# A fourth buffer in the ring of expert blocks for most of the last stage

## The reference, cut to what matters

```
def chunk(args):
    tc, ec, gc = args
    u_sel = expert_u[ec]
    a = jax.nn.gelu(jnp.einsum('cd,chkd->chk', tc, u_sel).astype(jnp.float32), approximate=False)
    w = (gc * a).astype(tc.dtype)
    return jnp.einsum('chk,chkd->cd', w, expert_v[ec])
```

## Time and profile before

| what | value |
|---|---|
| median of 3 timed runs | 1953.23 us |
| lowest and highest of them | 1952.56 and 1955.71 us |
| the profiled execution, its own time | 1951.24 us |
| its span, first to last instruction | 1949.3 us |
| busy: PE, DVE, ACT, POOL | 1940.0, 1664.4, 1122.1, 664.4 us |
| HBM traffic over the span | 290 GB/s |

### The profile page before, as it was taken

The page is one execution under the profiler, slowest core; times in us unless marked ns, Lnnn a source line. Parts: engine busy times, 40 slices in busy tenths (PEclk is TensorE's granted clock), DMA queues, the critical chain, the costliest instruction groups (busy, mean ns, idle before and its releaser), DMA issues.

```text
span 1949.3 us, 32645 instructions
## 1 busy us (share of the span) xinstructions
PE 1940.0 (100%) x11722; PEld 1765.4 (91%) x11722; DVE 1664.4 (85%) x2523; ACT 1122.1 (58%) x1589; POOL 664.4 (34%) x409
## 2 busy tenths in 40 slices
PE   9999999999999999999999999999999999999999
PEld 8899989998988888999999999999888888888887
DVE  8777778777888777999999999998888988888887
ACT  7565556555677455656665665655555455555555
POOL 0301110011000001887777877686222221333220
PEclk9999999999999999999999999999999999999999
DMA  6745654565455556999999999999999999999997
GB/s 246 252 160 194 204 191 159 188 204 194 162 173 192 185 173 228 336 341 341 334 334 341 345 326 355 336 384 356 358 364 387 381 374 371 381 376 381 371 379 270
DMA packets 137575, 566.50 MB, mean 291 GB/s; under 512 B 44008, under 2 KB 52080, under 8 KB 88112
## 3 DMA queue, kind: packets, MB, share of 16 engines
q1 hardware_dynamic: 87152, 414.05, 58.1%
q0 software_dynamic: 49936, 149.49, 22.9%
q10 hardware_dynamic: 432, 2.37, 0.3%
HBM read 548.31 MB, written 16.88 MB: 290 GB/s over the span
## 4 chain that ended last, share of the span: by engine, by line
PE 90%; DMA 4%; DVE 3%; ACT 1%; issue 1%; DVEq 0%; ACTq 0%; SPq 0%
PE psum L946 25%; PE psum L923 16%; PE psum L616 15%; PE psum L928 10%; PE psum L620 8%; PE psum L602 3%; PE psum L601 3%; PE psum L606 3%; DMA raw<-v_rows 2%; DMA arena<-u_cols 1%; ACT whi L479 1%; DVE xr L487 1%; DVE wlo L487 1%; PE psum L818 1%; PE psum L1000 0%
## 5 line engine op out<-in xcount | busy, mean ns | idle before, releaser
L473 DVE TENSOR_TENSOR wlo<-raw,whi 128x1024 fp32r<-128x1024 f32 x242 | 296.1, 1231 | 110.3 <-PE psum L620 72.2
L923 PE MATMUL psum<-xr,whi 128*128 128x384 f32 x2048 | 380.9, 337 | 0.0
L946 PE MATMUL psum<-whi,xr 128*128 128x512 f32 x1512 | 364.0, 390 | 0.3 <-DVE xr L1888 0.2
L923 PEld LDWEIGHTS psum<-xr,whi 128*128 128x128 f32 x2048 | 351.2, 188 | 0.5 <-ACT whi L479 0.2
L946 PEld LDWEIGHTS psum<-whi,xr 128*128 128x128 f32 x1512 | 283.6, 188 | 60.4 <-ACT whi L479 1.0
L479 ACT ACTIVATE whi<-raw 128x2048 fp32r<-128x2048 f32 x168 | 320.9, 1910 | 27.5 <-DMA raw<-v_rows 17.0
L616 PE MATMUL psum<-xr,whi 128*128 128x512 f32 x1296 | 330.2, 397 | 0.0
L466 ACT ACTIVATE whi<-raw 128x1024 fp32r<-128x1024 f32 x244 | 250.4, 1054 | 110.7 <-DMA raw<-stream 52.9
L1388 POOL DMA_INDIRECT arena<-v_rows,small x64 | 142.2, 2222 | 399.5 <-DVE arena L1852 396.0
L616 PEld LDWEIGHTS psum<-xr,whi 128*128 128x128 f32 x1296 | 232.6, 189 | 43.6 <-issue 0.2
L487 DVE TENSOR_TENSOR wlo<-raw,whi 128x1024 fp32r<-128x1024 f32 (+1 forms) x126 | 197.6, 1573 | 23.4 <-issue 19.9
(11 more groups left out here) (283 smaller groups left out, 3236.4 us busy)
## 6 DMA issues: line engine op xcount, KB each, us to landing
raw<-stream SPq DMA_DIRECT2D x244, 512.0 KB, 3.3
raw<-v_rows SPq DMA_DIRECT2D x85, 1024.0 KB
raw<-u_cols SPq DMA_DIRECT2D x84, 1024.0 KB
arena<-v_rows SPq DMA_DIRECT2D x43, 1024.0 KB, 7.9
arena<-u_cols SPq DMA_DIRECT2D x42, 1024.0 KB, 6.8
gates<-arena POOLq DMA_DIRECT2D x8, 1536.0 KB, 9.7
small<-gates SPq DMA_DIRECT2D x62, 192.0 KB, 8.2
arena<-x_t SPq DMA_DIRECT2D x4, 544.0 KB, 6.6
```

The costliest lines, as they stand in the source:

```text
L473: nc.vector.tensor_tensor(wlo[:, k % 2 * HALF:(k % 2 + 1) * HALF], raw[:, s * HALF:(s + 1) * HALF], f(whi[:, s * HALF:(s + 1) * HALF]), AL ...
L923: mm(bank(at, 0, 2 * TD), hi_w[:, c * P:(c + 1) * P], z_all[:, :, c, 0:TD // TS, :], start=c == 0, stop=False)
L946: last = mm(at[:, (b * 4 + j * 2 + n) * 512:(b * 4 + j * 2 + n + 1) * 512], weights, src, start=begin, stop=end, skip_group_check=True)
```

## The change

From block 144 on (block 16 of the V stage) the ring has a fourth slot, the first 2048 columns of arena, which held weight chunks that are used up by then. Blocks up to 143 keep their slots. Block 144 goes to the new slot, 145 to slot 0, 146 to 1, 147 to 2, 148 to the new one again, and so on. In SP's loop the turn n = 140 loads blocks 143 and 144; every later turn loads block n + 4 in place of n + 3. The waits for a block's load count the loads of its slot with a function, since a slot's count is no longer a quotient of the block's number.

```
-        slots = [raw[:, 0:D], raw[:, D:2 * D], top.take(D)]
+        slots = [raw[:, 0:D], raw[:, D:2 * D], top.take(D), arena[:, 0:D]]
+        DEEPER = F_V - F_U + 16
+
+        def slot(b):
+            return b % 3 if b < DEEPER else (3, 0, 1, 2)[(b - DEEPER) % 4]
+
+        def loads(b):
+            s = slot(b)
+            return sum(slot(a) == s for a in range(2, b + 1)) if s == 2 else sum(slot(a) == s for a in range(3, b + 1))
...
-        block_landed = [sem(f"block_landed{s}") for s in range(3)]
+        block_landed = [sem(f"block_landed{s}") for s in range(4)]
...
         def hi_block(act, b):
-            act.wait_ge(block_landed[b % 3], 16 * (b // 3 + (b % 3 == 2)))
-            nc.scalar.activation(whi[:, b % 2 * D:(b % 2 + 1) * D], slots[b % 3], ACT.Copy).then_inc(hi_done, 2)
+            act.wait_ge(block_landed[slot(b)], 16 * loads(b))
+            nc.scalar.activation(whi[:, b % 2 * D:(b % 2 + 1) * D], slots[slot(b)], ACT.Copy).then_inc(hi_done, 2)
...
             def load_block(b):
-                sp.dma_start(slots[b % 3], u_blocks[b] if b < B_U else v_blocks[b - B_U]).then_inc(block_landed[b % 3], 16)
+                sp.dma_start(slots[slot(b)], u_blocks[b] if b < B_U else v_blocks[b - B_U]).then_inc(block_landed[slot(b)], 16)
...
             for n in range(B_U + B_V - 3):
                 sp.wait_ge(lo_done, 2 * F_U + 2 * n + 2)
-                load_block(n + 3)
+                if n + 3 < DEEPER:
+                    load_block(n + 3)
+                if n + 4 >= DEEPER and n + 4 <= B_LAST:
+                    load_block(n + 4)
```

More of the change, by code:

```diff
@@ L484, in lo_part @@
                 dve.wait_ge(half_done, 2 * F_U + 2 * b - 2)
-            halves = [t.rearrange("p (z n) -> p z n", z=2) for t in (slots[b % 3], f(whi[:, b % 2 * D:(b % 2 + 1) * D]))]
+            halves = [t.rearrange("p (z n) -> p z n", z=2) for t in (slots[slot(b)], f(whi[:, b % 2 * D:(b % 2 + 1) * D]))]
             at = slice(parts[0], parts[-1] + 1)
@@ L491, in last_hi_half @@
         def last_hi_half(act, z):
-            act.wait_ge(block_landed[B_LAST % 3], 16 * (B_LAST // 3 + (B_LAST % 3 == 2)))
-            nc.scalar.activation(last_hi[:, z * HALF:(z + 1) * HALF], slots[B_LAST % 3][:, z * HALF:(z + 1) * HALF],
+            act.wait_ge(block_landed[slot(B_LAST)], 16 * loads(B_LAST))
+            nc.scalar.activation(last_hi[:, z * HALF:(z + 1) * HALF], slots[slot(B_LAST)][:, z * HALF:(z + 1) * HALF],
                                  ACT.Copy).then_inc(hi_done, 1)
@@ L498, in last_lo_half @@
             dve.wait_ge(hi_done, 2 * F_U + 2 * B_LAST + z + 1)
-            nc.vector.tensor_tensor(last_lo[:, at], slots[B_LAST % 3][:, at], f(last_hi[:, at]), ALU.subtract).then_inc(lo_done, 1)
+            nc.vector.tensor_tensor(last_lo[:, at], slots[slot(B_LAST)][:, at], f(last_hi[:, at]), ALU.subtract).then_inc(lo_done, 1)
         @block.sync
```

## The result

The changed kernel takes 1957.33 us (median of 22 runs, 1949.83 to 1966.75), the kernel before on the same chip 1954.01 us (22 runs, 1948.31 to 1958.12). The ratio is 1.0019, with a 95% interval of 1.0011 to 1.0026. The change is a small loss: some 3.7 us by the ratio where 0.7 us of gain was forecast, and the time lies 1.1 us above the range.

A forecast was written before the change was run, and what follows sets the result against it. PE was taken to bound the kernel, with 2.1 us lost in the value stage. -1.10 + 0.4 = -0.7 gave 1950.5 us profiled, a median of 1952.5; the eight-in-ten range was 1949.6 to 1956.2.

The forecast's parts named there:

- What the lead removes: Value stage from block 16: loads one block (4.535 us) earlier end all load waits, saving 1.10 us of PE.
- Buffers, rotation and slot at no cost: Slot in arena, semaphores and indices: same instruction counts, no new wait on any engine, cost 0.
- The gates at the switch: Where two blocks go out in one turn, near 1417: gates about 2.4 us late, costing PE 0.4 us (0 to 0.87).
- charged nothing more: Gates loads 2 and 3 after the switch: backlog worked off, lateness under the 2.32 us PE didn't feel, cost 0.
- the gates as the bound: Rival, DVE's gates wait at line 1883: backlog stays one block, half of 18 waits cost 7.8 us, 1959.9 us; chance 0.12.
- each stall lets DMA catch up by as much: Argument against the gates becoming the bound: the surplus is a single block, so the debt is paid after a few stalls.
- The ring order: SP's DMA ring: descriptors go in order, so gates can't overtake the added block, making its 2.8 us certain.
- The 425 GB/s: DMA rate for a core streaming alone: the extra block would be gone after an estimated 23 us, same sum.
- The eaten lead: Rival: DMA at share 0.98 can't get ahead, so ACT's load waits and the stalls stay; 1953.2 us; chance 0.21.
- More lost than shown: Rival: slow timed runs hide late loads; with all 2.1 us of the stage gone too, 1949.1 us; chance 0.06.
- the three stalls by blocks: Value stage: PE losses of 0.42, 0.32 and 0.36 us traced to late block loads, forecast to go, 1.10 us.

The follow-up runs named there:

- e1: The change with SP issuing the gates load ahead of the block load of the same turn, four slots: 1950.79 us, ratio 0.9983 to the kernel before.
- e2: The kernel before, three slots, with the gates load issued ahead of the block load in the same turn: 1952.45 us, ratio 0.9994.
- e4: The change with the gates loads issued by ACT on its own queue, four slots: 1950.13 us, ratio 0.998 to the kernel before.
- e6: The kernel before, three slots, with the gates loads issued by ACT on its own queue: 1953.26 us, ratio 0.9997.
- e3: The change's four slots and rotation, but loads only three blocks ahead as before: 1953.26 us, ratio 0.9993 to the kernel before.
- e8: The change with gates ahead of the block only in the last 16 turns that load gates: 1953.19 us, ratio 1.0003 to the kernel before.
- e10: The change with gates ahead of the block load, measured again beside the unedited change on one chip: 1950.91 us, ratio 0.9982 to the kernel before.
- e7: The change unedited, measured again for a second profile: 1955.08 us, ratio 1.0003 to the kernel before.
- e9: The change unedited, measured once more beside the gates-ahead version on the same chip: 1955.32 us, ratio 1.0015 to the kernel before.
- e5: The change with a fifth slot from block 48 of the stage, loads five ahead, gates still behind the block: 1955.06 us, ratio 1.0005.

## Why the prediction was wrong

*What the lead removes: right.* Waits for blocks fell from 23 to 4.7 us, and none of the stalls after the switch is one of them. The term was -1.10. With gates out of the way the slot gives about 2 us by e1 against e2 (0.0011 of the time), and e4 against e6 (0.998 against 0.9997) says some 3; both are differences of intervals that overlap, so 1.10 isn't excluded.

*Buffers, rotation and slot at no cost: right.* e3 has them without the lead at 0.9993, in an interval that holds 1.

*The gates at the switch: right in place, a little small in price.* The forecast was gates about 2.4 us late and 0.4 us lost, bounds 0 and 0.87. Measured: 1.70 us late at 1430.46, and 0.75 us lost 13 us later, once DVE's backlog reached PE.

*The failed step: later gates loads "charged nothing more".* After the switch 0.57, 2.35 and 2.43 us were lost in the profiled execution, 5.35 in all, where 0 was charged. The prediction took the gates' lateness to be the backlog of one extra block, and let the price end with it. That the backlog is worked off was right. The 8th part of the gates is back from 8.61 us at the switch to 6.55 four loads later, at 1455; from 1430.46 to 1502 no wait for gates in this trace is over 0.22 us; and two blocks are on the way at an issue, as before. But the price did not end. Already before, gates landed at the edge of their lead, 8.2 us at the median against some 8.6, and the longest were late by one part in sixteen, not by a longer queue in front. With the fourth slot the waits come back in the same stretches as before, longer: 34.6, 36.0 and 29.8 us in the change's three traces (longest 4.1, 4.8 and 4.0) against 15.1 before and 15.9 in e3 (2.4 and 2.2); only e8, with the change's order in all but the last turns, stayed at 18.2 (2.3). That the loss is these waits is shown: e1, e4 and e10 keep the slot and the lead, have almost no wait for gates, and gain.

Why the waits are longer with the fourth slot is not shown. The 8th part comes 0.4 to 0.5 us later at the median (6.95, 6.96 and 6.88 in the change's traces, 6.47 before), which is much for a transfer without slack; the last part was some 1.4 us later at its worst (12.6 and 12.7 against 11.2), but e3 had a 12.2 with loads three ahead. Nor do the gates make each other late through their two buffers, as the chain's pair of 8.39 and 12.59 suggests: SP issued the second load straight behind the block of its turn, when its buffer had been free for 3.1 us, and its lead of 8.68 us was whole. Where DVE works off a backlog without a pause, a late load does shorten the next one's lead, to 7.6 and 7.9 us in two cases of e7 (loads of 1439.44 and 1550.98).

*The rival that came true is the gates as the bound.* Its place (now line 1894) and its sign held. Its condition, a backlog that stays at one block, didn't come about, and its price was another: it took 0.87 us a stall and six stalls before it showed; two stalls of 2.35 and 2.43 us, with waits of 3.94 and 4.07, made most of the loss. Against it stood that "each stall lets DMA catch up by as much". Windows of e7 around its stall of 1566 (columns as in the earlier trace rows) show why that is only half true:

```profile
1566.00:1567.00 1.00, 0.35 (x2) 0.31 (x3) 1.00 (x3) 0.46 (x1) 0.41 (x1) 1.00 0.07 28
1567.00:1568.00 1.00, 1.00 (x5) 0.81 (x4) 1.00 (x1) 0.00 (x0) 1.00 (x1) 0.77 0.06 25
1568.00:1569.00 1.00, 1.00 (x3) 0.79 (x3) 1.00 (x3) 0.00 (x0) 1.00 (x1) 0.50 0.05 20
1569.00:1570.00 1.00, 1.00 (x4) 0.73 (x3) 1.00 (x3) 0.00 (x0) 0.60 (x1) 0.50 0.43 66
```

DMA did empty its queue, but then it stood at 20 to 28 GB/s for three us: a slot comes free through DVE's low half, and DVE had itself just been held by the gates. So part of the time that the stall bought is lost again.

*The ring order* that was cited from the Trainium skill ("DMA: Bandwidth & Descriptors", Queues, rings and completion order) is borne out: gates put ahead of the block land in 5.1 us at the median, behind it in 8.9. The prediction weighed it at the switch alone; the order counts all through the stage, and with three slots too (5.2 and 8.2). The 425 GB/s that the prediction takes from HBM Reference of the Trainium skill stand there in Specifications (TRN2), not in Access; nothing hung on them.

*The eaten lead* did not happen: the waits for blocks went. *More lost than shown* may hold a grain of truth, hidden under the loss: with a stage at its pace, e1 and e4 gain 0.0017 and 0.002 of the time, 3.3 and 3.9 us, where the profiled execution of before lost 2.1 us in the stage. The intervals, some 2 us to either side, don't settle it.

In sum, for the profiled executions: of the 2.1 us that the stage lost before, the three stalls by blocks are gone as forecast, and so is the one by gates; +0.4 came out as +0.75, and the 0 for all later gates as +5.35. That is 571.4 + 0.1 + 0.75 + 5.35 = 577.6 us for the stage, as measured. By the ratios of its three measurements the change lost 3.7, 0.6 and 2.9 us. In e7 and e9 it came to 1955.08 and 1955.32 us, inside the range, so that the first lies outside is in part chance; but none of the three shows the gain that was forecast.

Left open: what holds up the last part of a load, and why late gates come in bouts. DVE's waits cluster in stretches that begin near 1500, 1610, 1720 and 1830 in the traces before and after alike, so the cause is likely something that both kernels do; no experiment tried what. Also open is how much the end of the stage adds by itself (e8) and what a fifth slot costs in time (e5): their intervals are wider than the effect.

The version to keep is the fourth slot with the gates ahead of the block (0.9983 and 0.9982) or from ACT's queue (0.998); by its interval each beats the kernel before, and e10 beats the change on one chip. The queue of ACT was measured once.

## What to carry to other kernels

A deeper prefetch helps the stream that it is for, and can cost a just-in-time transfer that shares its queue: before adding a buffer, list what is issued behind the big loads, and set each one's own lead (here 8.7 us, given by the turn in which SP issues it, though its buffer stood free 3 us earlier) against its longest landing, not its median. Issue the small, urgent transfer ahead of the large, early one. When a landing is late, see whether all of its parts are late or one: at both switches here, where a block more stood in front, all of them were. A wait that a pipeline rides out at 2.4 us can cost more than 2 us at 4, so a sum of waits says less than the longest of them.

## What was not expected of the hardware

The stall of e7 cost more than PE's idle time. PE's timeline of e7 there:

```profile
1566.65 3.06 PE L957 MATMUL psum<-whi,xr 128*128 128x512 f32 x8 [2.87 <-DVE xr L1899]
1569.50 2.67 PE L957 MATMUL psum<-xr 128*128 128x512 f32 x8
1572.01 2.21 PE L957 MATMUL psum<-whi,xr 128*128 128x512 f32 x9
```

After 2.87 us of idle PE the granted clock went to 0.77 and then 0.50, the level of 1.2 GHz (windows above), while PE was at work again. The sixteen matmuls from 1566.65 took 1572.01 - 1566.65 = 5.36 us. In the changed kernel's first profile the sixteen behind the shorter idle of 1.66 us, from 1779.94 to 1784.10, took 4.16, with the granted clock at 1.00 throughout. So the longer stall cost another 1.2 us in these alone.
